# The first norm computed token by token before the transposes, its residual copy spread into the first projections, and the context tile fetched and transposed earlier

## What is computed

```python
def first_block(x, meta, norm_mix_w, w_in, ...):
    h = concatenate([meta, x], axis=1)                     # 528 tokens of 1024
    u = rms_norm(h, norm_mix_w[l])                         # h * rsqrt(mean(h*h) + eps) * w
    proj = u @ w_in[l]                                     # forget, gq, gk, fk, fq, fv, gv, gate ...
    mixed = concatenate([forgetting_attention(...), hgrn2_recurrence(...)]) @ w_out[l]
    h = h + mixed
    u = rms_norm(h, norm_ffn_w[l])
    h = h + (silu(u @ w_ffn_gate[l]) * (u @ w_ffn_up[l])) @ w_ffn_down[l]
    return rms_norm(h, norm_final_w)[:, N_META:]
# the second part also reads ctx_2 (256 tokens of 1024), normed and projected
```

## Time and profile before

| | us |
|---|---|
| median of 3 runs | 2877.87 |
| lowest and highest | 2873.15, 2878.06 |
| the profiled execution | 2870.0 |
| its span, first to last instruction | 2868.2 |

### The profile page before, as it was taken

How to read it: one execution, slowest core, us unless ns; L and a number is a source line. 1 busy time by engine, 2 the same in 40 slices (tenths; PEclk the granted TensorE clock), 3 DMA queues, 4 the chain that set the end, 5 groups by cost and what they waited for, 6 DMA issues and landing times.

```text
span 2868.2 us, 35556 instructions
## 1 busy us (share of the span) xinstructions
PE 2578.5 (90%) x14214; PEld 2173.3 (76%) x14214; DVE 1572.0 (55%) x2811; ACT 1077.9 (38%) x1833; POOL 257.4 (9%) x120
## 2 busy tenths in 40 slices
PE   2988886999996899998699999999799999799997
PEld 2877775888885787777588888887678887677876
DVE  3655664577666577777755443444445556533333
ACT  4433442322224455555421111112455666322223
POOL 0211200000000122222000000000122321000000
PEclk6999988999998999999799999999799999899999
DMA  2211102354441111111033333331212322122231
GB/s 76 59 39 43 45 30 98 126 184 161 139 159 37 52 37 38 37 38 50 17 125 102 108 108 113 107 110 45 63 43 57 71 58 58 59 98 78 99 99 52
DMA packets 250463, 223.70 MB, mean 78 GB/s; under 512 B 36996, under 2 KB 222122, under 8 KB 250298
## 3 DMA queue, kind: packets, MB, share of 16 engines
q1 hardware_dynamic: 250298, 221.43, 25.1%
HBM read 219.18 MB, written 2.22 MB: 77 GB/s over the span
## 4 chain that ended last, share of the span: by engine, by line
PE 75%; DVE 13%; ACT 8%; issue 4%; DMA 1%; SPq 0%; DVEq 0%; ACTq 0%
PE ps L350 23%; PE ps L351 22%; PE ps L352 22%; DVE FR L506 2%; ACT FR L501 1%; DVE hT L2020 1%; PE ps L2216 1%; DVE FA L447 1%; PE ps L981 1%; PE ps L631 1%; ACT whi L375 1%; ACT FA L1941 1%; PE ps L1852 1%; DVE Ul L455 1%; PE ps L2227 1%
## 5 line engine op out<-in xcount | busy, mean ns | idle before, releaser
L350 PE MATMUL ps<-Uh,whi 128*128 128x512 f32 (+2 forms) x2480 | 899.8, 363 | 66.2 <-DVE Ul L455 22.6
L351 PE MATMUL ps<-Ul,whi 128*128 128x512 f32 (+2 forms) x2480 | 884.4, 357 | 0.0
L352 PE MATMUL ps<-Uh,wlo 128*128 128x512 f32 (+2 forms) x2480 | 883.3, 356 | 0.0
L350 PEld LDWEIGHTS ps<-Uh,whi 128*128 128x128 f32 x2480 | 483.2, 195 | 148.2 <-issue 45.7
L352 PEld LDWEIGHTS ps<-Uh,wlo 128*128 128x128 f32 x2480 | 482.7, 195 | 63.7
L351 PEld LDWEIGHTS ps<-Ul,whi 128*128 128x128 f32 x2480 | 483.8, 195 | 60.0
L375 ACT ACTIVATE whi<-raw 128x1024 fp32r<-128x1024 f32 (+2 forms) x211 | 297.4, 1410 | 571.0 <-PE ps L352 570.7
L386 DVE TENSOR_TENSOR wlo<-raw,whi 128x2048 fp32r<-128x2048 f32 (+2 forms) x128 | 250.4, 1957 | 308.4 <-ACT whi L375 308.4
L350 PE MATMUL ps<-FR,whi 128*128 128x512 f32 (+1 forms) x768 | 286.4, 373 | 27.8 <-DVE FR L506 22.3
L351 PE MATMUL ps<-FR,whi 128*128 128x512 f32 (+1 forms) x768 | 283.9, 370 | 0.0
L352 PE MATMUL ps<-FR,wlo 128*128 128x512 f32 (+1 forms) x768 | 283.7, 369 | 0.0
(11 more groups left out here) (267 smaller groups left out, 3155.0 us busy)
## 6 DMA issues: line engine op xcount, KB each, us to landing
FA<-in_ada_w_dram SPq DMA_DIRECT2D x192, 256.0 KB, 2.8
raw<-in_ffn_w_gate_up_dram SPq DMA_DIRECT2D x44, 1024.0 KB, 5.1
raw<-in_ffn_w_down_dram SPq DMA_DIRECT2D x24, 768.0 KB, 4.2
raw<-in_w_in_dram SPq DMA_DIRECT2D x29, 512.0 KB, 3.8
raw<-in_da_wqkv_dram SPq DMA_DIRECT2D x24, 512.0 KB, 3.6
raw<-in_na_wqkv_dram SPq DMA_DIRECT2D x24, 512.0 KB, 3.7
raw<-in_w_ffn_gate_dram SPq DMA_DIRECT2D x11, 1024.0 KB, 5.2
raw<-in_w_ffn_up_dram SPq DMA_DIRECT2D x11, 1024.0 KB, 5.3
```

Source lines behind the costliest of these rows:

```text
L350: e.matmul(out, ah, bh, start=start, stop=False)
L351: e.matmul(out, ah, bl, start=False, stop=False)
L352: return e.matmul(out, al, bh, start=False, stop=stop)
```

## The change

- **Loads.** `ident`, `meta` and the four tiles of `x` are loaded first, then the norm's weight (as a broadcast row for meta and as eight rows), then weight chunks 0 and 1, then everything else. The table's write to memory moves behind the third chunk's fetch.
- **Norm by token.** ACT squares each tile of 128 tokens by 1024 features as it comes, with the sum over the row as a by-product (tokens are in partitions, so no product with ones); one Ln and one Exp on five columns give the roots of all tokens. ACT scales tiles 0 and 1, DVE tiles 2 and 3 and meta. Then TensorE transposes the scaled tiles, and ACT and DVE write Uh and Ul out of PSUM, multiplying with the weight there. One table set with Ln and Exp is loaded once at the start; the gating of the condition is written with Exp and a reciprocal in place of Sigmoid.
- **Residual copy.** The eight blocks of raw `x` that hT needs are transposed later, in eight steps `keep` between the first projections, each taking a bank of the ring. The work on small vectors is a step `later` behind gq; the clearing of AT is a step `clear` behind fq. Chunk 0's low part is written by POOL.
- **Forget group.** All 24 products of 512 tokens come first, then the 24 of 16 tokens.
- **Context.** Its two loads are issued during the output product, behind the second w_out chunk. Four blocks are transposed behind the last w_out product, four behind the norm's sum. ACT copies one of them after each high part of the norm, blocks 0 and 7 first (they lie in banks 1 and 0, where the first gate products go). The squares come after the norm.

The diff, cut to its core:

```diff
+        self.xt, self.xs = (t[:, 0:4096].rearrange("p (t d) -> p t d", t=4) for t in (FA, flat))
+        self.xm, self.xms = FA[0:NM, 4208:5232], flat[0:NM, 4096:5120]
+        self.norm_sums, self.norm_roots = FA[:, 4096:4101], FA[:, 4104:4109]
+
+        self.wrow, self.rows = self.raw[0][0:NM, 1024:2048], self.raw[1][:, 1024:1280]
...
+        self.pad, self.rotf = FA[:, 5792:6048].rearrange("p (b d) -> p b d", b=2), FA[:, 6048:6176]
...
+        self.fl = FA[0:8, 4208:5792].rearrange("p (a b) -> p a b", a=3)
...
 def prelude_sync(K, e, w):
...
+    e.dma_start(K.ident[:, :], A["ident"]).then_inc(*K.dma("ident"))
+    e.dma_start(K.xm, A["meta"]).then_inc(*K.dma("xm"))
+    for t in range(4):
+        e.dma_start(K.xt[:, t, :], A["x"][0, t * P:(t + 1) * P, :]).then_inc(*K.dma(f"x{t}", "x"))
+    e.dma_start(K.wrow, A["norm_mix_w"].broadcast_to([NM, D])).then_inc(*K.dma("wrow"))
...
+        e.dma_start(K.rows[r:r + n, 0:P], flat.rearrange("(r p) -> r p", p=P)).then_inc(
+            *K.dma("first_rows" if name == "norm_mix_w" else "rows", name))
+        if name == "norm_mix_w":
+            fetch_chunk(K, e, w)
+            fetch_chunk(K, e, w)
+    e.dma_start(K.rows[0:96, P:2 * P], A["ada_b_2"].rearrange("l (j p) -> (l j) p", p=P)).then_inc(*K.dma("rows", "ada_b"))
+    e.dma_start(K.fbias[0:8, :], A["fox_f_bias"].rearrange("a h -> h a")).then_inc(*K.dma("fbias"))
...
-    e.dma_start(K.xm, A["meta"]).then_inc(*K.dma("xm"))
+        e.dma_start(K.lam4[:, i, :], A[nm].broadcast_to([P, 64])).then_inc(*K.dma("lams", i))
...
-    w.wait_ge(*K.at("rpb_in"))
-    e.dma_start(K.rpbd.ap().rearrange("(b q) c -> q b c", b=2), K.pad[0:120, :, :]).then_inc(*K.dma("rpb_out"))
-    fetch_chunk(K, e, w)
-    fetch_chunk(K, e, w)
...
+
+    ident = K.ident
+    w.wait_ge(*K.at("ident"))
+    w.wait_ge(*K.at("first_rows", "norm_mix_w"))
+    b = K.hold(w, 7, ("cols", 0))
+    e.transpose(b[:, 0:8], K.rows[0:8, 0:P], ident[0:8, 0:8]).then_inc(*K.ev("cols_turned", 0))
+    for t in range(2):
+        w.wait_ge(*K.at("rows_act", t))
+    for t in range(2, 4):
+        w.wait_ge(*K.at("rows_dve", t))
+    for c in range(KC):
+        o = K.hold(w, c, ("norm_lo", "x", c, 0))
+        for t in range(4):
+            i = e.transpose(o[:, t * P:(t + 1) * P], K.xs[:, t, c * P:(c + 1) * P], ident[:, :])
+        i.then_inc(*K.ev("rows_turned", c))
+    o = K.hold(w, 0, ("norm_lo", "x", KC, 0))
+    w.wait_ge(*K.at("rows_dve", 4))
+    for c in range(KC):
+        i = e.transpose(o[:, c * NM:(c + 1) * NM], K.xms[:, c * P:(c + 1) * P], ident[0:NM, 0:NM])
+    i.then_inc(*K.ev("rows_turned", KC))
+    b = K.hold(w, 1, ("cols", 2))
+    w.wait_ge(*K.at("rows", "ada_b"))
+    e.transpose(b[:, 0:NROWS], K.rows[0:NROWS, 0:P], ident[0:NROWS, 0:NROWS])
+    e.transpose(b[:, 128:224], K.rows[0:96, P:2 * P], ident[0:96, 0:96]).then_inc(*K.ev("cols_turned", 1))
+
...
+def prelude_scalar(K, e, w):
+    e.preload_act_table_set("natural_log_exp_and_others")
...
+    e.activation(K.xms, K.xm, ACT.Square, accum_out=ss[0:NM, 4:5]).then_inc(*K.ev("rows_square", 4))
...
+        e.activation(K.xs[:, t, :], K.xt[:, t, :], ACT.Square, accum_out=ss[:, t:t + 1]).then_inc(*K.ev("rows_square", t))
+    w.wait_ge(*K.at("rows_square", 3))
+    e.activation(r, ss, ACT.Ln, bias=K.eps[:, :], scale=1.0 / D).then_inc(*K.ev("norm_ln", "x", 0))
+    w.wait_ge(*K.at("norm_ln", "x", 0))
+    e.activation(r, r, ACT.Exp, scale=-0.5).then_inc(*K.ev("norm_root", "x", 0))
+    w.wait_ge(*K.at("norm_root", "x", 0))
+    for t in range(2):
+        e.activation(K.xs[:, t, :], K.xt[:, t, :], ACT.Copy, scale=r[:, t:t + 1]).then_inc(*K.ev("rows_act", t))
+    split_hi(K, e, w)
+    w.wait_ge(*K.at("cols", 0))
     for c in range(KC):
...
+        w.wait_ge(*K.at("rows_turned", c))
+        halve_scalar(K, e, K.bank(c), K.Uh[:, c, 0:512], ("norm_hi", "x", c, 0), K.cp(col("norm_mix_w", c)))
+    w.wait_ge(*K.at("rows_turned", KC))
+    halve_scalar(K, e, K.bank(0)[:, 0:128].rearrange("p (c t) -> p c t", t=NM), K.Uh[:, :, 512:528], ("norm_hi", "x", KC, 0))
...
+def prelude_later_scalar(K, e, w):
+
+    w.wait_ge(*K.at("const", 2))
...
-    e.activation(sg[:, 0:16], K.cols[:, ROWS["c_2"][0]:ROWS["c_2"][0] + 16], ACT.Sigmoid).then_inc(*K.ev("cond_sigmoid"))
+    w.wait_ge(*K.at("cols", 2))
+    e.activation(sg[:, 0:16], K.cols[:, ROWS["c_2"][0]:ROWS["c_2"][0] + 16], ACT.Exp, scale=-1.0).then_inc(*K.ev("cond_exp"))
...
-    root_scalar(K, e, w, "x", (SX, SM))
-    norm_scalar(K, e, w, "x", ((0, 528),), lambda c, i: K.zero[:, :])
...
+    w.wait_ge(*K.at("cols_turned", 0))
+    e.tensor_copy(K.cols[:, 0:8], K.bank(7)[:, 0:8]).then_inc(*K.ev("cols", 0))
+    r = K.norm_roots
+    w.wait_ge(*K.at("norm_root", "x", 0))
+    for t in range(2, 4):
+        e.tensor_scalar(K.xs[:, t, :], K.xt[:, t, :], r[:, t:t + 1], None, ALU.mult).then_inc(*K.ev("rows_dve", t))
+    w.wait_ge(*K.at("wrow"))
+    e.scalar_tensor_tensor(out=K.xms, in0=K.xm, scalar=r[0:NM, 4:5], in1=K.wrow, op0=ALU.mult, op1=ALU.mult).then_inc(
+        *K.ev("rows_dve", 4))
+    w.wait_ge(*K.at("cols", 0))
+    for c in range(KC):
+        w.wait_ge(*K.at("norm_hi", "x", c, 0))
+        halve_vector(K, e, K.bank(c), K.Uh[:, c, 0:512], K.Ul[:, c, 0:512], ("norm_lo", "x", c, 0), K.cp(col("norm_mix_w", c)))
+    w.wait_ge(*K.at("norm_hi", "x", KC, 0))
+    halve_vector(K, e, K.bank(0)[:, 0:128].rearrange("p (c t) -> p c t", t=NM), K.Uh[:, :, 512:528], K.Ul[:, :, 512:528],
+                 ("norm_lo", "x", KC, 0))
+    K.lo_i = 1
...
+def prelude_later_vector(K, e, w):
+    cols, lam, z, l4 = K.cols, K.lam, K.small, K.lam4
+    w.wait_ge(*K.at("cols_turned", 1))
+    e.tensor_copy(cols[:, 8:NROWS], K.bank(1)[:, 8:NROWS]).then_inc(*K.ev("cols", 1))
...
+    e.tensor_scalar(z[:, 0:16], z[:, 0:16], 1.0, None, ALU.add).then_inc(*K.ev("cond", 0))
+    w.wait_ge(*K.at("cond", 0))
+    e.reciprocal(z[:, 0:16], z[:, 0:16]).then_inc(*K.ev("cond", 1))
+    w.wait_ge(*K.at("cond", 1))
...
-    norm_vector(K, e, w, "x", (SX, SM), ((0, 528),), lambda c, i: K.cp(col("norm_mix_w", c)), lambda c, i: K.zero[:, :])
...
+def prelude_gpsimd(K, e, w):
+    split_lo(K, e, w, "wlo_pool")
+    w.wait_ge(*K.at("wlo_pool", 0))
...
+        yield "keep", j, 0
+        yield "keep", j, 1
         yield "gq", j, 0
+        yield "later", j, 0
...
+        yield "keep", j, 2
+        yield "keep", j, 3
         yield "gk", j, 264
+        yield "keep", j, 4
...
+        yield "keep", j, 6
+        yield "keep", j, 7
...
+        yield "clear", j, 0
...
+        project_first(K, e, w, "x", 1, wh, wl, ((o1, 0, 0, 512, ("x_ff", 0)),))
+        w.wait_ge(*K.at("norm_lo", "x", KC, 0))
+        project(K, e, o2[:, 0:NM], wh, wl, 0, 512, 528).then_inc(*K.ev("x_ff", 1))
...
+        b = K.xbank["keep", j, x] = spare()
+        o = K.hold(w, b, ("x_copied", x))
+        for t in range(4):
+            i = e.transpose(o[:, t * P:(t + 1) * P], K.xt[:, t, x * P:(x + 1) * P], K.ident[:, :])
+        i.then_inc(*K.ev("x_turned", x))
...
-MIXERS_SCALAR = {"split": (("split", 0.0),), "split_first": (("split", 0.0), ("split", 0.1)), "forget": (("forget", 0.8),),
+MIXERS_SCALAR = {"split": (("split", 0.0),), "split_first": (("split", 0.0),), "keep": (("keep", 0.1),), "later": (("later", 0.0),), "forget": (("forget", 0.8),),
...
+        w.wait_ge(*K.at("x_turned", x))
+        e.activation(K.hT[:, x, 0:512], K.bank(K.xbank["keep", j, x]), ACT.Copy).then_inc(*K.ev("x_copied", x))
...
+        w.wait_ge(*K.at("x_decay", 3))
...
-    e.preload_act_table_set("natural_log_exp_and_others")
...
+        w.wait_ge(*K.at("x_turned", KC - 1))
+        w.wait_ge(*K.at("lev"))
+        e.memset(K.AT, 0.0).then_inc(*K.ev("g_pick", 0, -1))
...
+    w.wait_ge(*K.at("norm_lo", "x", KC, 0))
...
+    w.wait_ge(*K.at("rows_turned", KC))
...
+    w.wait_ge(*K.at("rpb_in"))
+    e.dma_start(K.rpbd.ap().rearrange("(b q) c -> q b c", b=2), K.pad[0:120, :, :]).then_inc(*K.dma("rpb_out"))
...
+    context_tensor(K, e, w, range(0, 4))
     norm_tensor(K, e, w, "f0", (SX,))
+    context_tensor(K, e, w, range(4, 8))
...
-    norm_scalar(K, e, w, "f0", (SX,), lambda c, i: K.zero[:, :])
+    for c in range(KC):
+        w.wait_ge(*K.at("norm_scaled", "f0", c, 0))
+        e.activation(K.Uh[:, c, 0:512], K.st_tmp[:, c % 2, 0:512], ACT.Identity, bias=K.zero[:, :]).then_inc(*K.ev("norm_hi", "f0", c, 0))
+        context_scalar(K, e, w, (0, 7, 1, 2, 3, 4, 5, 6)[c])
...
-    for n in range(7):
-        fetch_chunk(K, e, w)
...
-def context_sync(K, e, w):
-    w.wait_ge(*K.at("norm_lo", "f0", KC - 1, 0))
+    fetch_chunk(K, e, w)
+    fetch_chunk(K, e, w)
+    w.wait_ge(*K.at("g_close", 3))
     for t in range(2):
         e.dma_start(K.ct[:, t, :], K.A["ctx_2"][0, t * P:(t + 1) * P, :]).then_inc(*K.dma(f"x{t}", "c"))
-
...
+    for n in range(5):
+        fetch_chunk(K, e, w)
...
+def context_bank(c):
+    return (c + 1) % 8
...
+        o = K.hold(w, context_bank(c), ("c_copied", c))
...
```

(21 more changed lines are left out.)

97 lines of the change are left out of this document (29 added, 68 removed).

## The result

The changed kernel takes 2823.69 us (median of 4 runs, 2823.27 to 2828.75) against 2876.97 us of the kernel before (4 runs, 2873.15 to 2878.06): a ratio of 0.9821 with an interval of 0.9804 to 0.9838, 53.3 us. The forecast was 2835, the range 2823 to 2849, so the time lies 11.3 under the forecast and 0.7 inside the range. By the spans of the two profiled executions, 2868.2 and 2821.7, the gain is 46.5, and 42.5 was worked out. Four later medians of the kernel before, each over 9 to 15 runs, are 2872.6, 2872.9, 2873.1 and 2870.1, and the changed kernel unedited came to 2823.98 beside the 2872.9, so that some 49 us is the better figure.

The account below looks back on a forecast made before the run. TensorE bounds the kernel; time is gained only where it idles or runs at lower clock. Terms 37.2 + 7.2 - 12.2 + 10.3 = 42.5 gave 2827.5 from the profiled 2870.0, 2835.4 from the median; forecast 2835, range 2823 to 2849.

Parts of the forecast that it names:

- Loads and norm: Kernel start: x loaded earlier and normed by token, so the first forget product starts at 22.8, not 60.05; gain 37.2.
- Forget group: First projection group: runs at full clock, 7.9 us instead of 15.1 at half clock; gain 7.2.
- rival F: From forget on, TensorE's clock stays at 0.50 and the kernel is slower, 2885 at 50 us; chance 0.02.
- rival D: Start: transposes leave the clock low, ending 1 us later and costing forget 1.95; time 2838, chance 0.10.
- From forget to table: Projections between forget and table: keeps and bank waits make it 35.0 us against 22.8; loss 12.2.
- gk's second half: After forget: waits 5.9 us for gq's bank, starting 16.1 us after the group's end.
- The low clock behind the wait: After the wait ahead of gk's second half: 3.9 us at half clock, costing 1.95.
- the wait ahead of fq: Projections before table: fq needs bank 5, freed late by DVE behind gk's chain; a wait of 0.9 us.
- The add held by POOL: gq's chain on DVE: POOL's pass, T + 9.4 to 11.8 after forget's end, holds the add.
- Behind table: From table on: every engine keeps its old order, so the shift of 32.2 is carried through.
- Context: Feed-forward start: earlier context loads remove the wait before the gate products; 12.25 less 1.95 of low clock, gain 10.3.
- The sum: Whole kernel: terms total 42.5 off the profiled execution's 2870.0, giving 2827.5.

Follow-up runs that it names:

- e1: Changed kernel with the context part undone (loads, transposes, copies and banks as before): 2835.02 us, ratio 0.9874.
- e3: Changed kernel with the eight keep blocks in banks 0, 2 and 3 instead of the ring: 2818.30 us, ratio 0.9816.
- e4: Changed kernel with the first up chunk's split moved ahead of the second norm's root: 2824.50 us, ratio 0.9837.
- e5: Changed kernel with the context squares moved behind the split of the first up chunk: 2816.97 us, ratio 0.9805.
- e7: Changed kernel with the four loads of x issued behind the small rows: 2837.30 us, ratio 0.9882.
- e8: Changed kernel with keeps in banks 0, 2 and 3 and the up chunk split ahead of the second norm's root: 2816.85 us, ratio 0.9811.
- e9: Changed kernel once more, unedited: 2823.98 us, ratio 0.9833.
- e12: Changed kernel with keeps in banks 0, 2 and 3 and the context squares behind the up chunk's split: 2812.11 us, ratio 0.9791.
- e6: Changed kernel with narrow products mixed between wide ones again in the forget group, starting after the meta parts: 2832.08 us, ratio 0.9862.
- e10: Changed kernel, forget group in its own order, but the first product waits for the meta tokens' parts: 2831.01 us, ratio 0.9851.
- e2: Kernel before with only the context part of the change: 2859.43 us, ratio 0.9956.
- e11: Kernel before with only its forget group reordered, 512-column products first, then the 16-column ones: 2867.12 us, ratio 0.9986.

## Why the prediction held, step by step

- **Loads and norm**: gain 40.0 instead of 37.2. x was in at 9.77, not 11.7: the last tile landed 6.7 us after its issue, where I had carried over the 8.4 of before, and the first issue was 0.2 earlier; the issues themselves took about what I had put. From there on the steps nearly kept their lengths: roots 1.7 us behind the last tile's start (1.8 predicted, with 0.2 for reading the sum that I had taken from no row; it took 0.19), scaling 2.3 (2.0), transposes 13.81 to 19.4 (5.55 us against 5.9), and 0.7 instead of 1.4 from there to the first product.
- **Forget group**: 8.5 us, 7.9 predicted, gain 6.6 of 7.2. I took the full clock from TensorE's unbroken work since the transposes, and the traces are in line with that, though they don't prove it. In all nine traces that go from the transposes into the group without a wait (the changed kernel, e1, e3, e4, e5, e7, e8, e9, e12) the 24 wide products ran at full clock; in the two with a wait of 1.17 and 1.31 us (e6, e10) the clock fell within 0.6 us. The order of the products, which I only mentioned against rival F, is not shown to carry the term. The size is in part luck: I took the 15.1 us at half clock as the old group's time and did not ask why the clock stayed low, and e2 ran the same products in 10.8. Against that execution the term would be 2.3.
- **Rule of the Trainium skill, "TensorE: Matmul & The Clock Gate", Part 4**, that transposes do not bring the clock up: rival D did not come. The 32 transposes took 5.04 us in e3, 5.55 in the changed kernel and 6.60 in e1, all between the 3.5 of 0.11 us each and the 6.7 of 0.21, so the pace changed among them each time, and the first wide product was at full clock.
- **From forget to table**: 35.2 us, 35.0 predicted. gk's second half started 16.0 us after the group's end, 16.1 predicted. The idle time ahead of it was 4.38, not 5.9, because the clock had already fallen at 27.9, among the last narrow products, and gq's products, that much slower, took up part of the difference; in e5, where that fall did not come, the wait was 5.30. The low clock behind the wait cost 1.7 (1.95 predicted), the wait ahead of fq was 1.21 (0.9).
- **The add held by POOL** came as in the earlier trace rows, 2.19 us; at 49.73 the same operation on 128x528 (L1377), with POOL idle, took 0.43. The Trainium skill, "SBUF — State Buffer", in the section on its two separate sides, describes an exclusive lock between GpSimd and DVE, for DVE's 2-port modes or two SBUF inputs, that the second of them waits out. The rows agree, as far as one pair can show: the add ends 0.3 us after POOL's pass. Which mode it ran in, no trace shows.
- **Behind table** the shift was to stay as it was. It grew by 2.6 us up to 217 us in stages that were not edited; e9 is 0.3 us behind the changed kernel at 50 us, 2.4 at 100 and 1.0 at 250, with the same instructions. I take the 2.6 for the clock's chance and no term.
- **Context**: 10.2 of 10.3. The gate products kept the full clock across a wait of 3.12 (I had left this open); the up product waited 5.15 (3.4 to 6) and started 13.1 us sooner by this part (12.25), but lost 2.95 by the low clock (1.95). The two misses cancel, so that the 10.2 is closer than its parts.
- **The size as a whole**: 46.5 by the spans where 42.5 was worked out: the start gave 2.8 more, the clock's chance 2.6, and the small misses took 1.4. The other 7 us of the 53.3 are in the reference: the profiled execution of the kernel before was 7 under the median of its runs, the changed kernel's profiled execution at its median. That is the largest miss of the forecast. The sum's 2827.5 was 3.7 above the profiled 2823.85; the 7.9 that I added, as if the changed kernel's median had to lie as far above its profiled execution, did not come, and that brought the time to within 0.7 us of the range's lower end.

The undone parts give the same picture by medians: loading x first 13.3, the forget group's order with its wait 8.1, the context 11.3. The rest of the 49, some 16 us, is the norm by tokens itself less the wait it brought with the keeps; it was not run by itself.

## What to carry to other kernels

Work each new wait out as a chain of engines: here the chain through gq's add, reciprocal and multiply gave the start of gk's second half to 0.1 us, and pointed to the edit that removes the wait. When a large gap closes, name the operation that is late next and move whatever stands needlessly ahead of it; the two edits found so gave another 11.6 us. Compare traces by the shift across the edited place, since whole executions of one kernel differ by 4 us and more. And look at every trace that holds the same unedited stage before explaining a difference there: e2, made for another question, took away the explanation that e11 alone seemed to prove.
